# Product-key experts on one core: loops written out, the token in PSUM, five row slots for each table

## The reference, cut to what matters

```python
PEER_HEADS = 8; N_KEYS = 128; PEER_TOPK = 16; PEER_BLOCK = 128; D_MODEL = 1024
def peer_ffn(h, w_q, sub_keys, u_tab, v_tab):
    q = (tok @ w_q).reshape(T, PEER_HEADS, 2, PEER_KEY_DIM // 2)
    s = jnp.einsum('thsk,snk->thsn', q, sub_keys)
    sv, si = lax.top_k(s, PEER_TOPK)                   # 16 best of 128 keys, on either side
    ...                                                # 256 sums of pairs, the 16 best of them: top_s, idx
    g = jax.nn.softmax(top_s, axis=-1)
    def block(args):                                   # 128 tokens, their indices and gates
        tb, ib, gb = args
        a = jax.nn.gelu(jnp.einsum('tkd,td->tk', jnp.take(u_tab, ib, axis=0), tb))
        return jnp.einsum('tk,tkd->td', gb * a, jnp.take(v_tab, ib, axis=0))
```

## Time and profile before

| | |
|---|---|
| median of three runs | 6189.84 us |
| profiled execution, span from first to last instruction | 6172.5 us |
| what lies between the span and the median | 17.3 us |
| PE, DVE, POOL, ACT busy | 4637.5, 2873.5, 2863.0, 450.7 us |
| gathered rows (queue q0) | 1342.34 MB of 1489.50 MB |
| chain that ended last, by engine | PE 39%, DMA 24%, issue 18%, DVE 9%, POOL 7% |
| mean granted TensorE clock | 0.938 of 2.4 GHz |

### The profile page before, as it was taken

The page is one execution under the profiler, slowest core; times in us unless marked ns, Lnnn a source line. Parts: engine busy times, 40 slices in busy tenths (PEclk is TensorE's granted clock), DMA queues, the critical chain, the costliest instruction groups (busy, mean ns, idle before and its releaser), DMA issues.

```text
span 6172.5 us, 45021 instructions
## 1 busy us (share of the span) xinstructions
PE 4637.5 (75%) x12847; PEld 2050.5 (33%) x12847; DVE 2873.5 (47%) x6890; ACT 450.7 (7%) x830; POOL 2863.0 (46%) x2569
## 2 busy tenths in 40 slices
PE   7999996566666766667789999956676766666666
PEld 3645544122222222222245555532222222222222
DVE  2241113665656656545312411146657566565543
ACT  1131010000000000000010400100000000000000
POOL 0000000676776767777500000017767777677774
PEclk9999998899999999999999999978999999999999
DMA  7101110899999999999851012119999999999996
GB/s 231 55 28 36 60 55 14 318 346 340 339 353 330 337 333 331 348 332 368 310 170 63 21 43 66 48 45 325 352 343 333 339 329 339 340 335 354 345 354 245
DMA packets 504201, 1489.50 MB, mean 241 GB/s; under 512 B 49632, under 2 KB 172976, under 8 KB 502578
## 3 DMA queue, kind: packets, MB, share of 16 engines
q0 software_dynamic: 368640, 1342.34, 59.6%
q1 hardware_dynamic: 126000, 140.54, 7.1%
q10 hardware_dynamic: 9346, 4.38, 0.3%
HBM read 1484.30 MB, written 2.79 MB: 241 GB/s over the span
## 4 chain that ended last, share of the span: by engine, by line
PE 39%; DMA 24%; issue 18%; DVE 9%; POOL 7%; ACT 1%; DVEq 1%; POOLq 0%; another core or an unknown queue 0%; PEldq 0%; PEld 0%; ACTq 0%; SPq 0%
DMA ring<-in_peer_v_dram,kt 16%; PE ps L468 10%; PE ps L822 10%; DMA ring<-in_peer_u_dram,kt 7%; POOL ring L1605 7%; PE ps L747 7%; DVE m_t L1506 3%; PE ps L511 2%; PE ps L754 2%; DVE ring L1517 2%; PE ps L552 1%; PE ps L699 1%; PE ps L679 1%; PE ps L627 1%; PE ps L499 1%
## 5 line engine op out<-in xcount | busy, mean ns | idle before, releaser
L822 PE MATMUL ps<-ring,m_t 128*128 128x512 f32 x5120 | 2655.2, 651 | 1270.3 <-DMA ring<-in_peer_v_dram,kt 913.1
L1605 POOL DMA_INDIRECT ring<-in_peer_u_dram,kt x1280 | 1363.8, 1065 | 2742.0 <-issue 1447.6
L1517 DVE CUSTOM_DVE_ANT_0 ring<-ring,m_t 128x1024 f32<-128x1024 f32 x1280 | 1553.7, 1225 | 1465.9 <-DMA ring<-in_peer_u_dram,kt 1403.3
L822 PEld LDWEIGHTS ps<-ring,m_t 128*128 128x128 f32 x5120 | 940.1, 201 | 2969.5 <-DMA ring<-in_peer_v_dram,kt 1797.0
L1605 POOL DMA_INDIRECT ring<-in_peer_v_dram,kt x1280 | 1498.6, 1171 | 519.1 <-issue 286.3
L468 PE MATMUL ps<-h_t,ring 128*128 128x128 f32 (+1 forms) x1536 | 426.1, 438 | 21.9 <-ACT h_t L895 14.6
L747 PE MATMUL ps<-h_t,ring 128*128 128x128 f32 (+1 forms) x1536 | 425.1, 435 | 11.7 <-issue 9.1
L1506 DVE TENSOR_SCALAR m_t<-cst,kt 128x128 f32<-128x128 f32 x1280 | 343.8, 367 | 21.5 <-issue 11.6
L468 PEld LDWEIGHTS ps<-h_t,ring 128*128 128x128 f32 x1536 | 235.1, 192 | 214.6 <-issue 209.7
L747 PEld LDWEIGHTS ps<-h_t,ring 128*128 128x128 f32 x1536 | 235.4, 191 | 199.6 <-issue 199.6
L1087 ACT ACTIVATE kt<-kt 128x16 f32<-128x16 f32 x80 | 17.3, 216 | 3439.7 <-DVEq L1533 1905.6
(11 more groups left out here) (212 smaller groups left out, 2592.1 us busy)
## 6 DMA issues: line engine op xcount, KB each, us to landing
ring<-in_w_ada_dram SPq DMA_DIRECT2D x48, 1024.0 KB, 6.7
ring<-in_w_in_dram SPq DMA_DIRECT2D x36, 1024.0 KB, 5.4
ring<-in_peer_u_dram,kt POOLq DMA_INDIRECT x1280
ring<-in_peer_v_dram,kt POOLq DMA_INDIRECT x1280
ring<-in_peer_wq_dram SPq DMA_DIRECT2D x16, 1024.0 KB, 5.5
ring<-in_tables_dram SPq DMA_DIRECT2D x10, 1024.0 KB, 4.8
ring<-in_w_out_dram SPq DMA_DIRECT2D x8, 1024.0 KB, 5.0
ring<-in_w_branch_c_dram SPq DMA_DIRECT2D x8, 512.0 KB, 6.5
```

The source lines that it names most:

```text
L822: mm = pe.matmul(y_acc[:, cols], diag[h % 2][:, k, :], rows_v[:, s, cols], start=n == 0, stop=n == EXPERTS - 1)
L1517: dve.tensor_tensor_reduce(rows_u[:, s, :], rows_u[:, s, :], tok_cur, 1.0, 0.0, ALU.mult, ALU.add, dots[:, n:n + 1]).then_inc(rows_u_free. ...
L1605: pool.indirect_dma_start(rows[:, s, :], None, table, bass.IndirectOffsetOnAxis(ap=idx, axis=0)).then_inc(came[s].sem, 16)
```

## The change

- Every `Fori` of the five streams becomes a Python loop, so that all instructions are written out and all semaphore values are constants. POOL's `carry_waits` goes, and each gather, product and V row counts rows through both layers (`row_number`).
- There are five slots for U rows and five for V rows. The fifth U slot is where `tok_cur` was, the fifth V slot is the half of `uq` that was unused in PEER. Of the last head's V rows 5 are issued ahead of the wait for the next indices, where it was 4.
- The token of a tile stays in PSUM, in one of two areas of two banks (`tok_acc`); DVE reads it there in `dot_products`. ACT no longer copies it.
- Key scores and outputs of PEER leave the table of turns and share one area of two banks, `key_acc`, in the order of `KEY_TURN`: scores of the next tile for both sides, then the output of this one. PE waits for `key_free` before each of the three.

```diff
-ROWS_U, ROWS_V = 4, 4
+ROWS_U, ROWS_V = 5, 5
...
+KEY_TURN = {name: n for n, name in enumerate(
+    [("key0", 0), ("key1", 0)]
+    + [x for j in range(TILES - 1) for x in (("key0", j + 1), ("key1", j + 1), ("out", j))] + [("out", TILES - 1)])}
...
-        rows_u = ring_flat[:, 0:ROWS_U * D].rearrange("p (s n) -> p s n", s=ROWS_U)
-        rows_v = ring_flat[:, ROWS_U * D:(ROWS_U + ROWS_V) * D].rearrange("p (s n) -> p s n", s=ROWS_V)
+        row_at = [ring_flat[:, n * D:(n + 1) * D] for n in range(8)]
+        rows_u = row_at[0:4] + [m_flat[:, 4096:4096 + D]]
+        rows_v = row_at[4:8] + [uq_flat[:, D:2 * D]]
...
-        tok_cur = m_flat[:, 4096:4096 + D]
...
+        key_acc = ps[:, 0:1024]
+        tok_acc = [ps[:, 1024:2048], ps[:, 2048:3072]]
...
-            with pe.Fori(0, LAYERS) as l:
+            for l in range(LAYERS):
...
+                def key_scores(name, queries):
+
+                    pe.wait_ge(key_free.sem, key_free.after(l, KEY_TURN[name]))
                     for g in range(PH):
-                        mm = pe.matmul(a[:, g * P:(g + 1) * P], queries[:, g, :], turned[:, 4 + g % 2, :],
+                        mm = pe.matmul(key_acc[:, g * P:(g + 1) * P], queries[:, g, :], turned[:, 4 + g % 2, :],
                                        start=True, stop=True)
-                    close_turn(name, mm)
...
+                    mm.then_inc(key_full.sem, 1)
+
+                def tokens(j, tile):
+
                     for k in range(KC):
-                        mm = pe.transpose(a[:, k * P:(k + 1) * P], tile[:, k, :], ident)
-                    close_turn(name, mm)
+                        mm = pe.transpose(tok_acc[j % 2][:, k * P:(k + 1) * P], tile[:, k, :], ident)
+                    mm.then_inc(tok_full.sem, 1)
...
-                def take_tokens(name, more, j):
-
-                    a = full(l, name, more)
-                    act.copy(tok_cur, a[:, 0:D]).then_inc(tok_ready.sem, 1)
...
                     if following:
-                        take_tokens("next_tok", j * 2, j + 1)
+                        act.wait_ge(tok_full.sem, tok_full.after(l, 2) + j)
...
-                    give_back(out)
+                    dve.drain().then_inc(key_free.sem, 1)
...
-                        s = n % ROWS_U
-                        dve.wait_ge(rows_u_in[s].sem,
-                                    rows_u_in[s].after(l, 16 * (n // ROWS_U + 1)) + j * (16 * EXPERTS // ROWS_U))
-                        dve.tensor_tensor_reduce(rows_u[:, s, :], rows_u[:, s, :], tok_cur, 1.0, 0.0, ALU.mult,
+                        m = row_number(l, j, n)
+                        s = m % ROWS_U
+                        dve.wait_ge(rows_u_in[s], 16 * (m // ROWS_U + 1))
+                        dve.tensor_tensor_reduce(rows_u[s], rows_u[s], tok_acc[j % 2], 1.0, 0.0, ALU.mult,
                                                  ALU.add, dots[:, n:n + 1]).then_inc(rows_u_free.sem, 1)
...
-                s = n % slots
-                pool.wait_ge(free.sem, free.after(l, n + 1 - slots) + j * EXPERTS)
-                carry_waits(pool, "pool")
-                pool.indirect_dma_start(rows[:, s, :], None, table, bass.IndirectOffsetOnAxis(
-                    ap=idx, axis=0)).then_inc(came[s].sem, 16)
+                m = row_number(l, j, n)
+                pool.wait_ge(free.sem, m + 1)
+                pool.indirect_dma_start(rows[m % slots], None, table, bass.IndirectOffsetOnAxis(
+                    ap=idx, axis=0)).then_inc(came[m % slots], 16)
```

More of the change, by code:

```diff
@@ L89, in turn_table @@
     order += [("gate", n) for n in range(3 * KC)] + [("out", n) for n in range(KC)] + ["norm2"]
[L90 to L95, removed]
+    order += [("pq", n) for n in range(2 * PH)]
     assert len(order) % 2 == 0, len(order)
@@ L408, in _ @@
                     load(l, CH_WIN + s, tables[s].rearrange("p (j n) -> p j n", j=STILES))
-                with sp.Fori(0, D // CW) as i:
+                for i in range(D // CW):
                     for s in range(3):
@@ L421, in _ @@
                     load(l, CH_OUT + s, cols_of(w_out, l, s * CW))
-                with sp.Fori(0, 2) as i:
+                for i in range(2):
                     for s in range(SLOTS):
@@ L735, in _ @@
                 carry_waits(pe, "pe")
-                with pe.Fori(0, D // CW) as i:
+                for i in range(D // CW):
                     for b in range(3):
@@ L768, in _ @@
                 root_mean(l, "norm2", KC)
-                with pe.Fori(0, 2) as i:
+                for i in range(2):
                     for s in range(SLOTS):
@@ L1034, in _ @@
                         take_values(v // TILES)
-                with act.Fori(0, D // CW) as i:
+                for i in range(D // CW):
                     for n in range(6):
@@ L1049, in _ @@
                 add_shift(l, KC, 3 * KC)
-                with act.Fori(0, 2) as i:
+                for i in range(2):
                     for n in range(8):
@@ L1328, in _ @@
                 dve.drain().then_inc(merged_credit.sem, 2)
-                with dve.Fori(0, D // CW) as i:
+                for i in range(D // CW):
                     for n in range(6):
@@ L1486, in select_part, with add_output @@
                         gates(j + 1)
-                def add_output(j, out, more):
-                    a = full(l, out, more)
+                def add_output(j):
+                    a = key_acc
+                    dve.wait_ge(key_full.sem, key_full.after(l, KEY_TURN["out", j] + 1))
                     for k in range(KC):
@@ L1626, in later_heads @@
                         v_row(j, n)
-                with pool.Fori(0, 1) as j:
+                for j in range(1):
                     pool.wait_ge(idx_ready.sem, idx_ready.after(l, 1) + j)
@@ L1633, in _ @@
                     later_heads(j)
-                with pool.Fori(0, TILES - 1) as j:
+                for j in range(TILES - 1):
                     pool.wait_ge(idx_ready.sem, idx_ready.after(l, 2) + j)
@@ L1640, in _ @@
                     later_heads(j + 1)
-                with pool.Fori(TILES - 1, TILES) as j:
+                for j in range(TILES - 1, TILES):
                     for n in range(LAST + ROWS_V, EXPERTS):
```

110 lines of the change are left out of this document (54 added, 56 removed).

## The result

The kernel after takes 5996.2 us (median of 4 runs, 5988.8 to 6000.4) against 6189.5 for the kernel before (6177.9 to 6198.8): a ratio of 0.969, 95% interval 0.9673 to 0.9708, so 193 us faster. Forecast were 5722, range 5610 to 5950. The sign was right, the size was not: 193 us came back and not 468. The profiled execution took 5996.05 us with a span of 5994.2, so the 17.3 us that I added for the difference of median and span were no offset but the scatter of runs.

What follows compares the result with a forecast made beforehand. POOL's gather issues, not the bytes, were taken to bound PEER. Shorter issues, fewer stalls and fewer jumps made 1746 us a layer, 464 us less for two layers, 468 with 4 us of loops: 5722 us, range 5610 to 5950.

Steps and rivals of the forecast that it cites:

- What bounded the kernel before: In PEER, POOL's issues of gathers, not the bytes, set the time: 396.5 us for a selecting tile.
- stretch: POOL issue time above the shortest, 0.94 us: 47 us a selecting tile, 456 in all; 38 a tile to go, 9 stay.
- Product with a PSUM operand: DVE's product of a U row with the token in PSUM: costs 6 ns more than 1.225 us, nothing in all.
- the key bank: Start of a PEER tile: PE's scores wait for DVE's addition, but hidden with 2.8 us to spare; nothing lost.
- the wait ahead of add_output: DVE's wait for PE before adding a tile's output, 5.5 us once a tile: stays mostly.
- Five slots: In a selecting PEER tile, POOL's stalls shrink: 9 us of waits for DVE and 3 of waits for PE.
- a fifth slot gives a fifth pair: Slot ring at a head's start: five pairs of 2.5 us against four of 2.87, each stall cut by 1 to 1.2 us.
- Loops: Loops written out: 9 us of POOL's jumps at tile ends (bounds 0 to 15), 4 us of jumps in loops elsewhere.
- DMA needs 328 plus what it is idle ... I add 5: Selecting PEER tile: 345 us by POOL's issues, with 5 us added for idle DMA engines: 350.
- the prediction is wrong if POOL's stalls grow by what the stretch gives back: Sign set beforehand against the forecast: POOL's waits in PEER grow by the issue time saved.
- Rival (b): In PEER memory does not sustain 409 GB/s, only 370: 266 us less, 5925 us; chance 0.09.
- (d): DVE becomes the bound, its product reading PSUM at a lower rate: +100 us in the mean, 6290 us; chance 0.03.

Runs made afterwards that it cites:

- late output: The kernel after, five slots, with DVE adding the previous tile's output behind head 2, not head 0, and PE's turned output in the free token bank: 5964.7 us, 0.9636.
- bare increments: Kernel after with light products, no V matmuls: PE only waits and increments for each V row, 5871.2 us; with seven unawaited increments more a row, 5956.8 us.
- gathers alone: Kernel after with products over 64 of 1024 elements and V matmuls over 64 of 512 columns (but a tile's first row), all gathers kept: 5921.2 us.
- PE's signals only: Kernel after with light products and no V matmuls; PE only waits for each V row and gives its slot back: 5871.2 us with five slots.

## Why the prediction missed

- **What bounded the kernel before:** right in what stretches the issues, and too strong in what that costs. With the token in PSUM the mean issue fell to 0.96 to 0.98 us; forecast were 9 us of stretch left in a selecting tile, measured 7. But with four slots 388 us less of stretch gave 124 us: the next limit lay much nearer behind the issues than my sum had it.
- **Product with a PSUM operand, the key bank:** right. 1.219 us; PE's scores at the start of a tile wait 2.8 us for DVE's addition, and are ready before the diagonals end. But the wait ahead of add_output, which I let stand at 5.5 us, grew to 11 us and more. The late output took it away; that run is 33 us faster.
- **Five slots:** 12 us a tile were forecast. With the token in SBUF they gave 95 us, 9.5 a tile; with it in PSUM 7 us in all. The step failed by being added to the other: "a fifth slot gives a fifth pair" costs out a stall of fixed length, and the stalls grew as the engines filled.
- **Loops:** 13 us in the sum, 61 measured (45 to 77), with the key bank. The bound of 15 us for the tiles was too low: PEER lost 37. The jump is some 15 of it by the earlier trace rows; the other 22, and what lies outside PEER, I can't place.
- **The step that failed:** "DMA needs 328 plus what it is idle ... I add 5". The sum left 17 us of stalls in a selecting tile and added 5 for idle DMA engines, 350 in all. The tile takes 378 us with 52 of stalls, and 374 with nearly no work behind the gathers. The rate itself, 409 GB/s, was no mistake: the gathers hold 410 over 70 us. What fails is that the slots come back in time. Where the DMA engines are full PE finishes late: its drain takes 9 to 15 us and not 2.0, V slots and the tile's output come late, POOL stalls (331 us for V slots, 129 before) and the DMA engines run dry. That it is PE's instructions that are held back, and not memory, is shown in the runs with the bare increments, 0.70 us for one of 0.05; for the kernel after itself it is a conclusion from them and from its drains. The sentence "the prediction is wrong if POOL's stalls grow by what the stretch gives back" names what came.
- **Rival (b):** its signs came, short issues and 350 to 370 GB/s, but not its reason, since memory delivers 410 over 70 us. Its number, 5925, lies 71 us below the measured time; that the gathers alone take 5921 is luck.
- The page "DMA: Bandwidth & Descriptors" of the Trainium skill (section "Where 436 GB/s comes from") led by my working to 6045 us, nearer than my forecast. Its 358 GB/s is no ceiling here: 70 us hold 410, and a slice of 147 us of the kernel with PE's signals only holds 387. The mean of PEER is 355 in the kernel after. The two numbers agree, but by these runs not for the page's reason.
- **Smaller slips of the working:** (d) has +100 us for heads of 51 us, where 80 heads that are 1 us longer give 80.

What is open: by what path a full set of DMA engines holds back instructions of PE and DVE. One rival above all stands untested. Each time here, also of the kernel before, is that of an execution whose instructions were recorded. The pattern of two equal steps of 0.70 us for an instruction, one in its recorded duration and one behind it, would fit a hold-up in writing down its start and its end, and so would the dependence on the number of instructions. No run leaves the recording out, so how much of the 331 us of V stalls would be there without it isn't known. Semaphore traffic instead of the number of instructions is another rival for the eight increments. A late fetch of instructions is not the cause in the place shown: no packet of the instruction queues moved between 2038 and 2050, and PE's increments were 0.15 us apart again from 2050.2, before the next such packet at 2050.6. Seven slots with PE's signals only came out 18 us slower than five; with two runs of each and overlapping intervals of the ratios (0.9491 to 0.9546 and 0.9439 to 0.9525) that may be nothing.

## What to carry to other kernels

A rate read from 10 us of a trace is not a floor: take the work behind the transfers out and time them alone before costing what a freed queue will bring. If they are slow even so, take out the instructions that give the slots back, too: here that told a late consumer (410 GB/s over 70 us without it) from a slow memory. When two changes relieve one queue, look for what lies right behind it; their gains don't add (124 and 95 us alone, 131 together). An output that one engine waits for at a tile's start can be taken a head or two later, which costs only a bank that is free then.

## Hardware behaviour that I had not expected

- With the DMA engines full (410 GB/s), instructions that have nothing to do with a transfer can be held back: a plain increment on PE takes 0.70 us and not 0.05, DVE's TENSOR_SCALAR starts each 1.40 us and not each 0.26. PE's drain takes 9 to 15 us with five slots and the token in PSUM, up to 24 with seven, and 2.0 in the kernel before.
- It grows with the number of PE's instructions: seven plain increments more for each V row cost 86 us over 1280 rows (5871.2 to 5956.8), and the hold-up set in after 13 us at 406 GB/s; with one increment a row the engines stayed full for 64 us. Whether the recording of instructions causes it is not shown.
- By the matmuls' own records nothing of this is seen: the last ends at 1484.95 and PE's drain at 1498. It shows in who waits for PE ("PEq" and the idle time of ACT, DVE and POOL), and in the durations of PE's semaphore instructions.
- Gathers of 4 KB rows held 410 GB/s on this one core for 70 us.
